# Query roots moved into the exponential and squares moved to ScalarE in the key-value and query stage of a transformer block kernel

## The reference, cut to what matters

```python
kvf = h @ kv_w                               # shared_kv, width 2 * 1024 + 16
k = rms_norm(kvf[..., :D], k_norm_g)         # per head of 64
v = kvf[..., D:2 * D]
dcum = cumsum(log_sigmoid(kvf[..., 2 * D:] + kv_b_f))
qg = h2 @ w_qg                               # fox_mixer
q = rms_norm(qg[..., :D], q_norm_g)          # per head of 64
gate = sigmoid(qg[..., D:])
logits = (q @ k.T) * 64 ** -0.5 + dcum[t] - dcum[s]   # causal
o = softmax(logits) @ v
y = (o * gate) @ w_o
```

## Time and profile before

| | |
|---|---|
| three runs | 1227.97, 1228.97, 1230.12 us; median 1228.97 us |
| profiled execution | 1227.58 us, of which the trace spans 1225.8 us |
| PE busy | 1159.6 us (95%), weight loads 1005.2 us (82%) |
| DVE, ACT, POOL busy | 840.1, 593.7, 226.4 us |
| mean granted TensorE clock | 0.964 of 2.4 GHz |
| chain that ended last | PE 73%, DVE 13%, issue 4%, DMA 4%, ACT 4% |

### The profile page before, as it was taken

One profiled execution on the slowest core, in us unless ns is written; L12 is line 12 of the kernel. 1 busy time (PEld: TensorE's weight loads), 2 busy tenths in 40 slices (PEclk: granted clock), 3 DMA queues, 4 the chain that ended last, 5 costly groups with the idle time before them and its releaser, 6 DMA issues.

```text
span 1225.8 us, 18090 instructions
## 1 busy us (share of the span) xinstructions
PE 1159.6 (95%) x7032; PEld 1005.2 (82%) x7032; DVE 840.1 (69%) x880; ACT 593.7 (48%) x866; POOL 226.4 (18%) x168
## 2 busy tenths in 40 slices
PE   5899899999999999999989999989898998999997
PEld 1687658889999877898889999868676987999986
DVE  3795554878997969797677767759869368544543
ACT  4763254455656346444464434355535347443532
POOL 1036300015666111010013113001030000221300
PEclk9999899999999999999999999989989579999999
DMA  8675640148776977876558877957857014656551
GB/s 333 251 291 206 240 164 1 53 166 293 244 267 243 364 258 258 302 229 240 172 199 265 276 272 285 367 172 273 278 177 265 22 36 122 187 178 196 175 201 73
DMA packets 124303, 263.43 MB, mean 215 GB/s; under 512 B 8297, under 2 KB 76465, under 8 KB 114001
## 3 DMA queue, kind: packets, MB, share of 16 engines
q1 hardware_dynamic: 121553, 254.56, 59.3%
q0 software_dynamic: 2688, 8.02, 2.2%
HBM read 261.50 MB, written 1.05 MB: 214 GB/s over the span
## 4 chain that ended last, share of the span: by engine, by line
PE 73%; DVE 13%; issue 4%; DMA 4%; ACT 4%; SPq 1%; POOL 0%; DVEq 0%; ACTq 0%
PE ps L1765 21%; PE ps L1766 20%; PE ps L1767 20%; DVE wl L579 3%; DVE acc L591 2%; DMA raw<-in_w_in_dram 2%; ACT wh L1278 1%; PE ps L2056 1%; PE ps L2042 1%; PE ps L2072 1%; PE ps L2364 1%; PE ps L1800 1%; DVE vg L1090 1%; PE ps L2377 1%; DMA raw<-in_b_w_qg_dram 1%
## 5 line engine op out<-in xcount | busy, mean ns | idle before, releaser
L579 DVE TENSOR_TENSOR wl<-raw,wh 128x2048 fp32r<-128x2048 f32 (+2 forms) x149 | 346.5, 2328 | 124.2 <-ACT wh L1278 123.6
L1278 ACT ACTIVATE wh<-raw 128x2048 fp32r<-128x2048 f32 (+2 forms) x149 | 280.9, 1890 | 147.0 <-DMA raw<-in_ffn_w_down_dram 53.8
L1765 PE MATMUL ps<-hh,wh 128*128 128x256 f32 (+1 forms) x1192 | 338.1, 284 | 7.1 <-DVE hl L727 3.3
L1766 PE MATMUL ps<-hl,wh 128*128 128x256 f32 (+1 forms) x1192 | 334.9, 281 | 0.0
L1767 PE MATMUL ps<-hh,wl 128*128 128x256 f32 (+1 forms) x1192 | 334.8, 281 | 0.0
L1765 PEld LDWEIGHTS ps<-hh,wh 128*128 128x128 f32 (+1 forms) x1192 | 223.9, 188 | 9.4 <-issue 5.5
L1766 PEld LDWEIGHTS ps<-hl,wh 128*128 128x128 f32 (+1 forms) x1192 | 223.9, 188 | 0.3
L1767 PEld LDWEIGHTS ps<-hh,wl 128*128 128x128 f32 (+1 forms) x1192 | 223.8, 188 | 0.2
L1765 PE MATMUL ps<-wh,hh 128*128 128x512 f32 (+1 forms) x352 | 140.3, 399 | 11.4 <-DVE wl L579 4.6
L591 DVE SCALAR_TENSOR_TENSOR acc<-au,cs,acc 128x2048 f32<-128x2048 f32 x56 | 140.8, 2513 | 12.7 <-DMA acc<-in_ada_b_dram 9.5
L2510 POOL TENSOR_TENSOR gl<-hid,gh 128x256 f32 (+1 forms) x66 | 82.7, 1254 | 343.7 <-ACT gh L1605 343.7
(11 more groups left out here) (322 smaller groups left out, 1604.1 us busy)
## 6 DMA issues: line engine op xcount, KB each, us to landing
au<-in_ada_w_dram SPq DMA_DIRECT2D x48, 1024.0 KB, 5.9
raw<-in_ffn_w_gu_dram SPq DMA_DIRECT2D x88, 512.0 KB, 4.7
raw<-in_w_up_dram SPq DMA_DIRECT2D x44, 512.0 KB, 4.8
raw<-in_ffn_w_down_dram SPq DMA_DIRECT2D x44, 512.0 KB, 4.5
au<-in_w_ada_dram SPq DMA_DIRECT2D x18, 1024.0 KB, 5.6
raw<-in_a_w_in_dram SPq DMA_DIRECT2D x32, 512.0 KB, 5.2
raw<-in_w_down_dram SPq DMA_DIRECT2D x22, 512.0 KB, 6.5
raw<-in_w_in_dram SPq DMA_DIRECT2D x16, 512.0 KB, 6.4
```

Source lines behind the costliest of these rows:

```text
L579: nc.vector.tensor_tensor(wl[:, u % RAW, 0:n], raw[:, u % RAW, 0:n], wh[:, u % RAW, 0:n].bitcast(F32), ALU.subtract).then_inc(lo_done, 1)
L1278: nc.scalar.activation(wh[:, u % RAW, 0:n], raw[:, u % RAW, 0:n], ACT.Copy).then_inc(hi_done, 1)
L1765: nc.tensor.matmul(to, lh, rh, start=start, stop=False, skip_group_check=True)
L1766: nc.tensor.matmul(to, lh, rl, start=False, stop=False, skip_group_check=True)
```

## The change

It does five things. (1) At the first place, `hi_part(13)` goes behind the evacuation of the queries on ACT and `take(13)` behind the rotary step on DVE. (2) The squares move from POOL to ACT, right behind the evacuations, and `root(R_KH)` goes behind `hi_part(QG + 1)` and the copy of `f_rows`. (3) The queries are evacuated straight into `qa` and are not scaled there: their root goes into the exponential's `scale` and into the maxima, `dcum` and 1 are multiplied by `rt` to make up for it, and the norm weights are applied per row when the turned copy is evacuated (`gcol`, a column). (4) PE turns key quads 0 to 3 behind QG+4, 4 to 7 behind QG+5, query quads 0 to 3 behind QG+6 and 4 to 7 behind QG+7; DVE and ACT follow in that order. (5) `qt_f` is cut in two halves, since its first half is now written while other data is still in the old place.

```diff
@@ DVE, first place
-            for u in (5, 6, 7, 8, 9, 10, 13):
+            for u in range(5, 11):
                 take(u)
 ...
                 dve.wait_ge(q_roped, t + 1)
+            take(13)
             take(W_UQ)
@@ DVE, second place
             take(QG + 4)
-            take(QG + 5)
             dve.wait_ge(cum_done, 1)
 ...
+            take(QG + 5)
             head_sums(qsq, R_QH, 2)
-            take(QG + 6)
-            turned_heads(kt_f, 0, (1, 3))
-            take(QG + 7)
+            turned_keys((1, 3))
+            take(QG + 6)
             head_rstd(R_QH)
             for t in range(NT):
                 c = R_AT[R_QH] + t * FH
-                to = qa[t][:, :, 0:FD]
-                link(nc.vector.tensor_tensor(to, q_st[:, t, :].rearrange("p (h c) -> p h c", h=FH),
-                                             bcast(rs[:, c:c + FH], 2, FD), ALU.mult))
-                nc.vector.tensor_tensor(to, to, bcast(gq[:, 0, :], 1, FH), ALU.mult)
-                nc.vector.memset(qa[t][:, :, FD + 1:FD + 2], 1.0)
-                nc.vector.tensor_copy(qa[t][:, :, FD], dcum[:, t, :]).then_inc(qa_ready, 1)
-            turned_heads(kt_f, 0, (5, 7))
+                nc.vector.tensor_tensor(qa[t][:, :, FD], dcum[:, t, :], rt[:, c:c + FH], ALU.mult)
+                nc.vector.tensor_copy(qa[t][:, :, FD + 1], rt[:, c:c + FH]).then_inc(qa_ready, 1)
+            turned_keys((5, 7))
+            take(QG + 7)
+            turned_queries((1, 3))      # tensor_scalar by gcol[0:FA, 2:3]
             take(WO)
-            turned_heads(qt_f, 8, (1, 3, 5, 7))
+            turned_queries((5, 7))
 ...                                    # fox_max(h), behind the two maxima
+                nc.vector.tensor_tensor(nmax[:, 2 * h:2 * h + 2], nmax[:, 2 * h:2 * h + 2],
+                                        rs[:, c:c + NT * FH].rearrange("p (t h) -> p t h", t=NT)[:, :, h],
+                                        ALU.mult).then_inc(fm_ready, 1)
@@ ACT
-            hi_part(13)
             act.wait_ge(w_used, 11)
 ...                                    # evacuations of rg, cqt, ckt and qk_st
+            hi_part(13)
 ...
-                if b == 3:
-                    root(R_KH)
 ...
+                if b == 1:
+                    for t in range(NT):
+                        act.wait_ge(evac, EVACS + 3 + t)
+                        nc.scalar.activation(ksq[:, t, :], k_st[:, t, :], ACT.Square).then_inc(head_sq, 1)
 ...                                    # hi_part(QG + 1) and the copy of f_rows
+            root(R_KH)
+            hi_part(QG + 6)
+            turned_keys((0, 2))
+            root(R_QH)
+            hi_part(QG + 7)
+            gates(2)
+            turned_keys((4, 6))
+            hi_part(WO)
+            turned_queries((0, 2))
+            gates(3)
+            hi_part(WO + 1)
+            turned_queries((4, 6))
 ...                                    # the fox loop's exponential
-                                         bias=nmax[:, 2 * h + t:2 * h + t + 1],
+                                         scale=rs[:, c:c + 1], bias=nmax[:, 2 * h + t:2 * h + t + 1],
@@ PE
-            queries_gates(2)
+            queries_gates(2, (0,))
 ...
             turn_heads(ka_rows, 0, range(4))
-            queries_gates(3, (0,))
+            queries_gates(2, (1,))
             turn_heads(ka_rows, 0, range(4, 8))
+            queries_gates(3, (0,))
+            pe.wait_ge(qa_ready, NT)
+            turn_heads(qa, 8, range(4))
             queries_gates(3, (1,))
-            pe.wait_ge(qa_ready, NT)
-            turn_heads(qa, 8, range(8))
+            turn_heads(qa, 8, range(4, 8))
@@ POOL
-            pool.dma_start(gq[:, 0, :], a["b_q_norm_g_2"][0].partition_broadcast(P)).then_inc(in_small, 16)
+            pool.dma_start(gcol[0:FD, 0:1], a["b_q_norm_g_2"][0].rearrange("(d c) -> d c", c=1)).then_inc(in_small, 16)
 ...                                    # and the same for k_norm_g_2
-                    nc.gpsimd.tensor_tensor(sq[:, t, :], src[:, t, :], src[:, t, :], ALU.mult).then_inc(head_sq, 1)
```

More of the change, by code:

```diff
@@ L230, in build @@
         bf = sb("bf", [P, FH])
-        gq = sb("gq", [P, 2, FD])
+        gcol = sb("gcol", [P, 3])
         fz = sb("fz", [P, 6, NT, FH])
@@ L317, in build @@
         ksq = in_r("ksq", 0, [P, NT, D])
[L318 to L320 removed]
+        qa = [in_h("qa0", 8.25, [P, FH, FA]), in_r("qa1", 48, [P, FH, FA])]
+        qsq = in_r("qsq", 56, [P, NT, D])
         prob_f = in_r("prob_f", 48, [P, 2, 384])
@@ L1184, in _, with turned_keys, turned_queries @@
             nc.vector.tensor_scalar(ka[:, :, :, FD + 1], dcum[:, :, :], -1.0, None, ALU.mult).then_inc(ka_ready, 1)
+            take(QG + 5)
             head_sums(qsq, R_QH, 2)
-            take(QG + 6)
-            def turned_heads(to, base, quads):
+            def turned_keys(quads):
                 for q in quads:
-                    dve.wait_ge(f_turned, base + q + 1)
-                    nc.vector.tensor_copy(to[:, 2 * q:2 * q + 2, :],
+                    dve.wait_ge(f_turned, q + 1)
+                    nc.vector.tensor_copy(kt_f[:, 2 * q:2 * q + 2, :],
                                           ps[0:FA, 4 + q % 4, :].rearrange("p (h t) -> p h t", h=2))\
                         .then_inc(ft_evac, 1)
-            turned_heads(kt_f, 0, (1, 3))
-            take(QG + 7)
+            def turned_queries(quads):
+                for q in quads:
+                    dve.wait_ge(f_turned, 8 + q + 1)
+                    nc.vector.tensor_scalar(qt_f[q // 4][:, 2 * (q % 4):2 * (q % 4) + 2, :],
+                                            ps[0:FA, 4 + q % 4, :].rearrange("p (h t) -> p h t", h=2),
+                                            gcol[0:FA, 2:3], None, ALU.mult).then_inc(ft_evac, 1)
+            turned_keys((1, 3))
+            take(QG + 6)
             head_rstd(R_QH)
@@ L1695, in _, with turned_keys @@
             nc.scalar.activation(f_rows[:, :], ps[0:FH, 4, 0:TOK], ACT.Copy).then_inc(f_copied, 1)
[L1697 to L1700, removed]
+            root(R_KH)
+            def turned_keys(quads):
+                for q in quads:
+                    act.wait_ge(f_turned, q + 1)
+                    nc.scalar.activation(kt_f[:, 2 * q:2 * q + 2, :],
@@ L1701, in turned_heads, with turned_queries @@
                                          ps[0:FA, 4 + q % 4, :].rearrange("p (h t) -> p h t", h=2), ACT.Copy)\
                         .then_inc(act_step, 1)
[L1704 to L1710, removed]
-                if b == 2:
-                    root(R_QH)
+            def turned_queries(quads):
+                for q in quads:
+                    act.wait_ge(f_turned, 8 + q + 1)
+                    nc.scalar.activation(qt_f[q // 4][:, 2 * (q % 4):2 * (q % 4) + 2, :],
+                                         ps[0:FA, 4 + q % 4, :].rearrange("p (h t) -> p h t", h=2), ACT.Copy,
+                                         scale=gcol[0:FA, 2:3]).then_inc(act_step, 1)
@@ L1713, in _, with queries @@
+            def queries(b):
                 act.wait_ge(w_used, split_no(QG + 2 * b + 1) + 1)
                 for t in range(NT):
-                    dst = q_st if b < 2 else sg
-                    take_evac(dst[:, t, (b % 2) * HALF:(b % 2 + 1) * HALF], ps[:, 2 * (b % 2) + t, :],
-                              ACT.Copy if b < 2 else ACT.Sigmoid)
-                if b == 0:
-                    act.wait_ge(f_pre, 1)
-                    nc.scalar.activation(e1, az, ACT.Exp, scale=-1.0).then_inc(f_act, 1)
-                    act.wait_ge(f_pre, 2)
-                    nc.scalar.activation(ln, e1, ACT.Ln).then_inc(f_act, 1)
@@ L1723, in _, with gates @@
-                if b == 2:
-                    turned_heads(kt_f, 0)
+                    take_evac(qa[t][:, 8 * b:8 * b + 8, 0:FD],
+                              ps[:, 2 * b + t, :].rearrange("p (h c) -> p h c", h=8))
+            def gates(b):
+                act.wait_ge(w_used, split_no(QG + 2 * b + 1) + 1)
+                for t in range(NT):
+                    take_evac(sg[:, t, (b - 2) * HALF:(b - 1) * HALF], ps[:, 2 * (b - 2) + t, :], ACT.Sigmoid)
+            z, az, e1, mn, ln, ls = (fz[:, j] for j in range(6))
@@ new lines, in _ @@
+            hi_part(QG + 2)
+            hi_part(QG + 3)
+            queries(0)
+            act.wait_ge(f_pre, 1)
+            nc.scalar.activation(e1, az, ACT.Exp, scale=-1.0).then_inc(f_act, 1)
+            act.wait_ge(f_pre, 2)
+            nc.scalar.activation(ln, e1, ACT.Ln).then_inc(f_act, 1)
+            hi_part(QG + 4)
+            hi_part(QG + 5)
+            queries(1)
+            for t in range(NT):
+                act.wait_ge(evac, EVACS + 11 + t)
+                nc.scalar.activation(qsq[:, t, :].rearrange("p (h c) -> p h c", h=FH), qa[t][:, :, 0:FD],
+                                     ACT.Square).then_inc(head_sq, 1)
@@ L2541, in _ @@
             start_acc(8)
[L2543 to L2552 removed]
+            start_acc(9)
```

(2 more changed lines are left out.)

31 lines of the change are left out of this document (12 added, 19 removed).

## The result

The changed kernel takes 1215.76 us (median of 4 runs, 1214.27 to 1217.73) against 1229.55 us (median of 4, 1227.97 to 1230.38): ratio 0.989, 95% interval 0.9872 to 0.9908. The forecast was 1191.5, its range 1184 to 1212. The sign was right, the time was 24 us off and outside the range.

The account below looks back on a forecast made before the run. PE was taken to bound the kernel, each gap costing itself and a stretch at half clock. Terms 4.3 + 8.4 + 6.8 + 18.0 = 37.5 us off 1227.6, plus 1.4 for the median: 1191.5 us, range 1184 to 1212.

Parts of the forecast that it names:

- Term A: First place: rg right behind unit 10 makes PE 7.4 us early; DVE's folds leave 4.3 us of gain.
- second rival: Gap before the last key turns reaches about 2.5 us, clock falls through the latent attention: 1235 us; one in twelve.
- Term B: Unit QG+1: with the key root moved PE begins 3.1 us earlier and the clock gives 5.3 us: 8.4 us.
- Term C: Way into the fox loop: first turn of probabilities comes 6.8 us earlier, 6.5 us behind QG+7.
- Term D: Fox loop: clock stays at 1.00 despite an entry gap of about 2.1 us; 29.7 us, not 47.7: 18.0 us less.
- The rest: Scale operand in the exponentials, small DVE products, gcol loads, POOL's queue: no cost taken, 3 us kept for the range.
- The first: Rival: the clock falls at the entry of the fox loop all the same, D is lost: 1210 us; chance 0.26.

Follow-up runs that it names:

- e7: Kernel before with one edit, the key root moved behind the copy of f_rows: 1199.88 us.
- e3: Changed kernel with 8 products of 512 columns into an unused bank before the fox loop's first turn of probabilities: 1194.86 us.
- e5: Changed kernel with ACT's hi_part(WO + 1) moved ahead of the gates of QG+7: 1194.21 us.
- e2: Changed kernel with the folds of tiles 21, 22 and 23 each moved one place later: 1208.73 us.
- e13: Kernel before with the key root moved and 7 products of 512 columns ahead of QG+0: five runs at 1199.0 to 1203.3 us, four at 1221.2 to 1225.6.
- e12: Changed kernel with the edits of e2 and e5, plus 10, 10, 20 and 7 products into unused banks ahead of four turns of xn: 1182.85 us.
- e16: Changed kernel with the edits of e2 and e5, plus 10, 10, 18 and 7 products into a bank the turns of xn overwrite: 1182.59 us.

## Why the prediction failed, step by step

**Term A, 4.3 us: 0.** PE was 7.2 us early at the projection's end, 7.4 as worked out (5.4 at its start, 1.8 by its clock, where I had 2.1). The fold of tile 21 ended at 161.56 (forecast 161.4), but tile 23 then took 6.6 us to land (issued 161.59, fold began 168.23), not 5.0: the copy ended at 171.4, not 169.9, and PE's gap was 3.6 us, not 2.3. That is the second rival's condition, and the clock did fall; but only for about 7 us, in which the first scores lost 2.2 us, and not through the attention, as its 43 us assumed. The five other profiled runs with this code had 2.65 to 3.94 us at the place, each with a fall there. The rule cited there (the Trainium skill, "TensorE: Matmul & The Clock Gate", Part 4: a transpose does not count as PE being busy in the way a matmul does) would have made a fall here the likely case. By that rule e7's entry, 7.7 us of turns and gaps from 932.0 to 939.7, should have fallen as well, and it did not. The rule's direction deserved more weight than I gave it.

**Term B, 8.4 us: 9.3** in the two traces. The mechanism was right: the moved root alone brought 7.4 to 7.9 us and left the gap of 1.2 us that I had worked out. What I had put at nothing, the squares on ACT and DVE no longer beside POOL, seems to have brought the other 1.4 us, and with it no gap was left at all.

**Term C, 6.8 us: 6.6.** Right, and so was ACT's chain (6.5 us; 6.49 from 933.29 to the first turn).

**Term D, 18.0 us: -0.3.** This is the step that failed: "one gap of about 2.1 us stays until the first turn", and that it would not bring the clock down. The gap was 1.9 us, and the clock fell to 0.50 at 939.7; with the gap filled (e3) or cut to 0.66 us (e5) it stayed at 1.00. I had made a limit out of three gaps, 2.56 us (fell) against 1.76 and 1.31 (did not). The limit does not exist: in the changed kernel the very gap of 1.76 us ahead of the last feed-forward stage is 1.77 us long, and the clock fell behind it (window 1018 to 1025, 0.52; before 1.00), and e7 stayed at 1.00 through 2.22 us. The size was right: the loop took 28.6 us in e3 (forecast 29.7) and 47.7 in after, 19.1 us. With the clock held the total was 1194.9 us, the forecast 1191.5.

**The rest, 0.** The exponentials of 128 columns with a scale operand take 0.09 us more, the quarter that I named. By form, in e7 (without it) and e5 (with it):

```profile
L1740 ACT ACTIVATE prob_f<-ps,nmax 128x128 f32<-128x128 f32 x16 | 5.8, 365 | 4.1 <-DVE nmax L1215 4.1
```

```profile
L1781 ACT ACTIVATE prob_f<-ps,nmax,rs 128x128 f32<-128x128 f32 x16 | 7.3, 457 | 4.2 <-DVE nmax L1224 4.0
```

The loop at 1.00 grows from 27.5 to 28.6 us, all of it behind the turn of head 10; at 0.50 it grows by 0.3 us alone. That the longer exponentials are the reason fits, but no run takes the scale out alone.

**What had no term.** 5.8 us went in code that is the same in both kernels: behind gaps of 2.56 us at both places, PE was at 0.50 for 10 us near 460 and 7 near 622 where before it was 7 and 3, and for 7 us near 1020 where before it did not fall. I take it for the clock's noise and no effect of the change, since e2's trace, with the same code there, has yet another pattern (0.50 for 3 and 7 us near 457, 3 near 616, 7 near 1013); but no kernel was profiled twice, so that is not shown.

**The rivals.** The first, 1210 us at 0.26, is what happened; it came out at 1215.8 with A's 4.3 us missing too. The gap of 2.1 us lay between gaps that had gone either way, so this rival should have had about half the chance, and the range had to reach it with A lost as well: 1227.6 + 1.4 - 8.4 - 6.8 = 1213.8. B and C are real gains; that the kernel came out faster as a whole is luck in part, since the runs of the kernel before that it was measured against all lie in the larger group.

## What to carry to other kernels

A gap ahead of a long stretch of thin PE work is priced by that stretch: here 1.9 us cost 21. Look for what makes the gap on the engine that PE waits for, and move it into that engine's idle time (one line, 21.6 us); where nothing can be moved, a few products without use hold the clock. Measure a change to such a kernel with the gap closed on both sides: between two groups 22 us apart, a median of three or four runs can show the clock's luck and not the change (e7 seems to bring 30 us, and brings about 8). And price a stretch at 0.50 by its own products only where PE sets the pace.

## What the runs showed of the hardware

The fox loop held 1.00 for all of its 28.6 us (e3), at 1.78 us a head. In the changed kernel, with the clock down at its entry, it held 0.50 for 41 us, at 3.41 us a head, with PE busy in all of the window shown, and came back to 1.00 only at 980.7, behind eight turns of `o_f` and 7 us before its end. The same program gave the longer time in some executions and the shorter in others (21 of 66 of the kernel before), and gaps equal to 0.03 us stood ahead of a loop at 1.00 (e7) and of one at 0.50 (e13). A gap's length alone predicts neither. The cleanest sample is the gap ahead of the last feed-forward stage: 16 profiled executions (before, after, and the experiments but e12 and e16) have it at 1.75 to 1.77 us, and behind it the clock fell in eight and stayed at 1.00 in eight.
